# Channel-major tiles for the convolved columns, and the convolution beside the tile that follows each

## The reference, cut to what matters

```python
(m_qk, m_v, m_o, m_gate, m_if, a_q, a_k, a_v, a_gate,
 i_q, i_w, i_k, c_q, c_gate) = split_in(rms_norm(x, g_pre) @ w_in)     # m_qk: 2048 columns
qk, conv_state = causal_conv(m_qk, zeros, conv_w, conv_b)   # 4 taps per channel along the tokens, then SiLU
m_out, (C, n, m) = mlstm_mixer(qk, m_v, m_o, m_if, b_if, head_norm, carry0, MLSTM_CHUNK)  # 4 heads x 256
# beside it: sparse attention over selected keys, and attention over 256 memory tokens
y = x + rms_norm(concat(m_out * silu(m_gate), a_out * ..., c_out * ...) @ w_out, g_post)
```

## Time and profile before

| what | value |
|---|---|
| median of 3 runs | 1882.44 us (1881.62 to 1884.41) |
| the profiled execution | 1877.01 us, its span 1875.3 us |
| granted TensorE clock over the span | 0.937 of full speed |
| second group, last tile read at | 1256.8 us |
| numerators of heads 0 to 3 begin | 1391.1, 1461.0, 1529.6, 1580.3 us |
| tiles of the output projection begin | 1647 us |

### The profile page before, as it was taken

The page is one execution under the profiler, slowest core; times in us unless marked ns, Lnnn a source line. Parts: engine busy times, 40 slices in busy tenths (PEclk is TensorE's granted clock), DMA queues, the critical chain, the costliest instruction groups (busy, mean ns, idle before and its releaser), DMA issues.

```text
span 1875.3 us, 20980 instructions
## 1 busy us (share of the span) xinstructions
PE 1679.8 (90%) x7801; PEld 1272.0 (68%) x7801; DVE 814.8 (43%) x1319; ACT 569.1 (30%) x876; POOL 673.4 (36%) x448
## 2 busy tenths in 40 slices
PE   6899999999999499998899999987658789799995
PEld 5677775677897376776688778865334455477774
DVE  6400010599929856755632161112465454501113
ACT  5522233222221233233222422224244443312221
POOL 3655531333333166766444444421110111033331
PEclk9999999999999699999999999998667788789997
DMA  6544431233344267766455544437404323542222
GB/s 214 160 134 130 142 101 56 71 105 108 92 120 144 77 196 231 221 197 211 122 154 165 149 134 117 147 125 230 93 29 152 107 68 107 192 160 85 83 78 106
DMA packets 139674, 249.01 MB, mean 133 GB/s; under 512 B 26504, under 2 KB 63308, under 8 KB 136296
## 3 DMA queue, kind: packets, MB, share of 16 engines
q10 hardware_dynamic: 66928, 122.86, 21.0%
q1 hardware_dynamic: 55920, 72.76, 12.2%
q0 software_dynamic: 16736, 52.18, 9.6%
HBM read 204.11 MB, written 43.66 MB: 132 GB/s over the span
## 4 chain that ended last, share of the span: by engine, by line
PE 73%; DVE 13%; DMA 5%; ACT 4%; issue 2%; POOL 1%; ACTq 1%; SPq 0%; DVEq 0%; POOLq 0%
PE acc L431 16%; PE acc L433 16%; PE acc L432 16%; PE acc L426 4%; PE acc L427 4%; PE ps_c L991 3%; PE acc L1722 2%; DVE arena L1669 1%; PE ps_c L2116 1%; PE acc L2111 1%; DMA arena<-z_prompt 1%; PE ps_a L1155 1%; POOL w_lo L389 1%; ACT z_tile L471 1%; PE ps_a L1224 1%
## 5 line engine op out<-in xcount | busy, mean ns | idle before, releaser
L389 POOL TENSOR_TENSOR w_lo<-w_raw,w_hi 128x1024 fp32r<-128x1024 f32 (+1 forms) x200 | 466.7, 2334 | 814.8 <-ACT w_hi L385 814.5
L431 PE MATMUL acc<-w_hi,x_hi 128*128 128x512 f32 (+1 forms) x1472 | 580.4, 394 | 8.8 <-DVE keep L925 5.3
L433 PE MATMUL acc<-w_hi,x_lo 128*128 128x512 f32 (+1 forms) x1472 | 565.9, 384 | 0.0
L432 PE MATMUL acc<-w_lo,x_hi 128*128 128x512 f32 (+1 forms) x1472 | 565.3, 384 | 0.0
L385 ACT CAST w_hi<-w_raw 128x1024 fp32r<-128x1024 f32 (+1 forms) x200 | 204.2, 1021 | 758.3 <-PE acc L427 716.6
L431 PEld LDWEIGHTS acc<-w_hi,x_hi 128*128 128x128 f32 x1472 | 278.8, 189 | 93.9 <-issue 28.0
L433 PEld LDWEIGHTS acc<-w_hi,x_lo 128*128 128x128 f32 x1472 | 278.1, 189 | 55.8
L432 PEld LDWEIGHTS acc<-w_lo,x_hi 128*128 128x128 f32 x1472 | 278.8, 189 | 51.4 <-issue 0.7
L426 PE MATMUL acc<-w_hi,x_hi 128*64 128x512 f32 (+1 forms) x368 | 141.4, 385 | 0.0
L427 PE MATMUL acc<-w_lo,x_hi 128*64 128x512 f32 (+1 forms) x368 | 140.9, 384 | 0.0
L2231 DVE TENSOR_TENSOR arena<-arena (+1 forms) x16 | 14.0, 887 | 176.8 <-ACT arena L464 176.8
(11 more groups left out here) (439 smaller groups left out, 1903.0 us busy)
## 6 DMA issues: line engine op xcount, KB each, us to landing
w_raw<-in_w_in ACTq DMA_DIRECT2D x136, 512.0 KB, 3.7
z_prompt<-z_tile ACTq DMA_DIRECT2D x68, 256.0 KB, 2.5
w_raw<-in_w_out ACTq DMA_DIRECT2D x32, 512.0 KB, 3.6
arena<-z_prompt SPq DMA_DIRECT2D x4, 2088.0 KB, 10.2
w_raw<-in_w_mem_kv ACTq DMA_DIRECT2D x16, 512.0 KB, 4.1
arena<-q_sample POOLq DMA_DIRECT2D x32, 256.0 KB, 4.0
arena<-z_prompt SPq DMA_DIRECT2D x10, 512.0 KB, 7.3
between<-z_prompt SPq DMA_DIRECT2D x10, 512.0 KB, 10.1
```

The source lines that it names most:

```text
L389: nc.gpsimd.tensor_tensor(out=w_lo[:, c % 2, :, 0:w], in0=w_raw[:, c % RAWS, :, 0:w], in1=w_hi[:, c % 2, :, 0:w].bitcast(F32), op=ALU.subt ...
L431: nc.tensor.matmul(acc[m][:, 0:w], xh, wh, start=first, stop=False)
L432: nc.tensor.matmul(acc[m][:, 0:w], xh, wl, start=False, stop=False)
L433: last = nc.tensor.matmul(acc[m][:, 0:w], xl, wh, start=False, stop=end)
```

## The change

The ten tiles of the second group are taken in another order, with the four convolved ones as the fifth to eighth. In these four, PE takes the weights as the stationary operand and the tokens as the moving one, so that a PSUM bank holds 128 channels by 512 tokens. ACT copies the bank to `z_tile` without scaling. Beside the tile that follows, DVE multiplies by the tokens' RMS factors (spread over all partitions at the start), keeps the last three tokens, and applies the taps; ACT takes SiLU after that tile's sixth chunk and stores 128 channels by 512 tokens to a new scratch `qk_prompt`. The heads load q and k from there, already turned and convolved. The tap weights are loaded with the first tables and turned between two tiles of the first group. `p_conv` is written from the kept tokens, in six DMAs of 4-byte elements.

```diff
+    B_ORDER = (4, 5, 6, 7, 0, 1, 2, 3, 8, 9)
 def tensor_tile
+                            if kind == "t":
+                                xh, xl = hi_t[:, k, 0:S], lo_t[:, k, :]
+                                wh, wl = (v[:, c % 2, i, m * P:(m + 1) * P] for v in (w_hi, w_lo))
+                                nc.tensor.matmul(acc[m][:, :], wh, xh, start=first, stop=False)
+                                nc.tensor.matmul(acc[m][:, :], wl, xh, start=False, stop=False)
+                                last = nc.tensor.matmul(acc[m][:, :], wh, xl, start=False, stop=end)
+                                continue
 def scalar_evacuate
+                if kind == "t" and m < MT:
+                    nc.scalar.copy(z_tile[:, m, :], acc[m][:, :]).then_inc(acc_read, 1)
+                    continue
 def scalar_tile
+                if c == CH - 2 and late is not None:
+                    late()
+        def tensor_late_consts(pe):
+            pe.wait_ge(*at("rstd_spread"))
+            pe.wait_ge(tables_in, 16 * N_TABLES)
+            for m in range(MT):
+                nc.tensor.matmul(ps_c[:, m * P:(m + 1) * P], conv_a[:, m * P:(m + 1) * P], ident[:, :], start=True, stop=True)
+            for k in range(KT):
+                last = nc.tensor.transpose(ps_b[:, k * (CK + 1):(k + 1) * (CK + 1)], conv_nat[:, k * P:(k + 1) * P],
+                                           ident[0:CK + 1, 0:CK + 1])
+        def vector_conv(dve, i, m):
+            k = 4 * i + m
+            dve.wait_ge(acc_read, acc_base(N_B0 + CT0 + i) + m + 1)
+            dlink(nc.vector.tensor_tensor(out=conv_a, in0=z_tile[:, m, :], in1=rstd_bc, op=ALU.mult))
+            nc.vector.tensor_copy(last_rows(k // 8)[:, k % 8, :], conv_a[:, S - CK + 1:S])
+            out = z_tile[:, m, :]
+            dlink(nc.vector.tensor_scalar(out, conv_a, conv_c[:, k, CK - 1:CK], None, ALU.mult))
+            for j in range(1, CK):
+                ins = nc.vector.scalar_tensor_tensor(out=out[:, j:S], in0=conv_a[:, 0:S - j],
+                                                     scalar=conv_c[:, k, CK - 1 - j:CK - j], in1=out[:, j:S],
+                                                     op0=ALU.mult, op1=ALU.add)
...
+        def scalar_conv(act, i):
+            for m in range(MT):
+                act.wait_ge(cv_tapped, k + 1)
+                nc.scalar.activation(z_tile[:, m, :], z_tile[:, m, :], ACT.Silu, bias=conv_c[:, k, CK:CK + 1]).then_inc(cv_silu, 1)
+            for m in range(MT):
+                act.wait_ge(cv_silu, k + 1)
+                act.dma_start(qk_p[k * P:(k + 1) * P, :], z_tile[:, m, :]).then_inc(z_stored[m], 16)
+        def sync_conv_state(sp):
+            sp.wait_ge(cv_tapped, 4 * NCT)
+            for half in range(2):
+                for j in range(CK - 1):
+                    sp.dma_start(O["p_conv"][0, 0, j, half * MW:(half + 1) * MW].rearrange("(k p) -> p k", p=P),
+                                 last_rows(half)[:, :, j], allow_slow_non_contiguous=True).then_inc(conv_out, 16)
 def sync_mlstm_head
-            for i, c in enumerate((C_QK, C_QK + MW, C_O, C_G, C_V)):
+            for i in range(2):
+                src = qk_p[i * MW + h * MD:i * MW + (h + 1) * MD, :].rearrange("(d p) t -> p d t", p=P)
+                sp.dma_start(qk_t[h % 2][:, i, :, :], src).then_inc(zh_in[h % 2], 16)
+            for i, c in enumerate((C_V, C_O, C_G)):
 def tensor_mlstm_head
-            pe.wait_ge(conv_silu, 4 * (h + 1))
+            pe.wait_ge(zh_in[h % 2], zh_count(h))
...
-                if h + 1 < H:
-                    tensor_conv_turn(pe, h + 1, i)
 block.vector, the loop over the second group's chunks
-            for _ in range(CH * NBT):
+            for i in range(CH * NBT):
                 next(prompt, None)
                 next(rows, None)
                 next(prompt, None)
+                t = i // CH - CT0 - 1
+                if 0 <= t < NCT and i % CH < MT:
+                    vector_conv(dve, t, i % CH)
```

More of the change, by code:

```diff
@@ L58, in hybrid_decoder_step @@
     NBT = C_IF // TN
+    NCT = 2 * MW // TN
+    B_ORDER = (4, 5, 6, 7, 0, 1, 2, 3, 8, 9)
+    CT0 = B_ORDER.index(0)
+    assert len(B_ORDER) == NBT and B_ORDER[CT0:CT0 + NCT] == tuple(range(NCT))
     N_Y0 = N_B0 + NBT
@@ L491, in tile_loop, with scalar_tile @@
                 body(n0 + 1)
-        def scalar_tile(act, n, kind, steps=NO_STEPS, often=False):
+        def scalar_tile(act, n, kind, steps=NO_STEPS, often=False, late=None):
             for c in range(1, CH + 1):
@@ L566, in hybrid_decoder_step @@
         gate_s = keep[:, 912:1040]
+        CK = 4
+        conv_nat = place(X_OFF, [2 * MW], CK + 1)
+        conv_a = place(X_OFF + 3112, [S])
+        conv_c = conv_cols[:, :].rearrange("p (k j) -> p k j", j=CK + 1)
+        last_rows = lambda half: small[:, 32 * half:32 * half + 24].rearrange("p (k j) -> p k j", j=CK - 1)
         POOL_PAGES = 2 * CH * IXT
@@ new lines, in vector_late_consts @@
+        def vector_late_consts(dve):
+            dve.wait_ge(rstd_ready, 2)
+            for m in range(MT):
+                last = nc.vector.tensor_copy(conv_a[:, m * P:(m + 1) * P], rstd(NU_MEM + m, P).broadcast_to([P, P]))
+            last.then_inc(reached("rstd_spread"), 1)
+            dve.wait_ge(*at("late_turned"))
+            nc.vector.tensor_copy(rstd_bc, ps_c[:, :])
+            nc.vector.tensor_copy(conv_c, ps_b[:, 0:KT * (CK + 1)].rearrange("p (k j) -> p k j", j=CK + 1)
+                                  ).then_inc(reached("late_copied"), 1)
+            dve.wait_ge(*at("late_copied"))
@@ L1462, in hybrid_decoder_step @@
         c_e = keep_m[:, 40:60].rearrange("p (m h) -> p m h", h=H)
[L1463 to L1475, removed]
+        mx_T = keep_m[0:H, 60:70]
+        bias_g = keep_m[0:H, 70:72]
+        m0_s = keep_m[0:H, 72:80]
+        a_T = keep_m[0:H, 80:88]
+        bn_o = keep_m[:, 88:96]
+        st_m = keep_m[:, 96:104]
+        aT8 = keep_m[0:NB, 104:108]
+        w_b = keep_m[0:R, 108:140].rearrange("p (h b) -> p h b", h=H)
+        batch_of = keep_m[0:R, 140:148]
+        head_rows = sb("head_rows", [P, H * P])
+        hr = head_rows[0:H, :]
+        rstd_bc = head_rows[:, :]
+        z_h = [place(M0, [2, MT, MD]), part(xl_free, 0, [2, MT, MD])]
         va = [place(M0 + 5120, [MT, MD + 2]), part(xl_free, 4096, [MT, MD + 2])]
         qk_t = [place(M0 + 7180, [2, 2, S]), part(xl_free, 5128, [2, 2, S])]
-        cv = [place(M0 + 6152, [S]), place(M0 + 6668, [S])]
         k_n = place(M0 + 9228, [MT, MD])
@@ L2429, in _ @@
             for n in range(N_B0, N_Y0):
-                scalar_tile(act, n, "b", steps)
+                i = n - N_B0
+                scalar_tile(act, n, tile_kind(n), steps,
+                            late=(lambda i=i: scalar_conv(act, i - CT0 - 1)) if CT0 < i <= CT0 + NCT else None)
             run(steps[0])
@@ L2469, in _ @@
             run(mem_s)
-            for u in range(4):
-                vector_conv(dve, 0, u)
             prep, pairs = vector_mlstm_s_prep(dve), vector_mlstm_s(dve)
@@ L2498, in _ @@
             for n in range(N_B0, N_Y0):
-                tensor_tile(pe, n, "b", steps)
+                tensor_tile(pe, n, tile_kind(n), steps)
             run(steps[0])
```

115 lines of the change are left out of this document (37 added, 78 removed).

## The result

The changed kernel takes 1860.14 us (median of 4 runs, 1854.18 to 1865.89), the kernel before 1883.43 beside it (4 runs); ratio 0.9875, 95% interval 0.9841 to 0.9909. It is faster by 23 us where 42 were forecast. The time lies inside the range that I gave, 2 us from its upper end, and outside the forecast's own 1828 to 1853. So places are compared inside the executions, and totals by the medians.

The account below looks back on a forecast made before the run. PE was taken to bound the second group, a chain of single waits the heads. Heads gain 55 us, the second group costs 13: 42 off the 1882.4 median gives 1840; own ends 1828 to 1853, range 1822 to 1862.

Parts of the forecast that it names:

- slower than before: Rival: p_conv's 4-byte stores, priced 25 us on SP's queue, delay the heads' constants and loads; 1885 or more, chance 0.04.
- The heads: Convolution units leave the heads: 18 us to head 0's numerator, 36 in heads 1 and 2, 1 in the memory stage; 55.
- 18 + 1: Head 0's numerator 18 us earlier (2.5 at the start, then 16.0), plus 1 from weights and constants turned before the memory stage.
- the 16.0: Inside head 0: four gains summed as head 1's units no longer alternate with the sample rows' preparation.
- the 36: Heads 1 and 2: both numerator spacings fall to head 3's 50.7, 37.1 us, taken as 36; bounds nothing and 37.1.
- The heads refill: Rival: DVE's normalisation, states' loads or table loads keep heads 1 and 2 near 60 us; 1858, chance 0.12.
- spacings over 58: Sign against the forecast: numerators of the heads over 58 us apart, where near 51 was expected.
- The second group: Added cost of 13 us: turned constants 2, sixth tile 8, seventh tile 2, ninth tile 1.
- 4 to 13: Sixth tile: bounds of an 8 us cost, as two convolutions are queued on DVE ahead of the sample rows' softmax.
- The turned constants: Before the index stage: four 128-wide products and 16 small ones cost PE 2 us; DVE's copies lie in a wait.
- the exchange of operands: Second group: matmuls and weight loads keep number and shape, only which operand stands still changes; priced 0.
- PE waits in the second group that sum to over 30: Sign against the forecast: PE's waits there total over 30 us; a 10 to 15 us softmax wait was expected.

Follow-up runs that it names:

- the store mended: Against the changed kernel, kept tokens are turned on PE, copied by ACT and stored as 48 rows of 512 bytes; 1838.05 us, 0.9774 of the kernel before.
- e_spread: Changed kernel with the six stores' 4-byte elements written 512 bytes apart in a scratch, p_conv itself not written; 1837.70 us, 0.9765 of the kernel before.

## Why the prediction was right and where it was wrong

**`p_conv`: the step that failed.** Under "slower than before" I gave the stores 25 us on the DMA engines, looked for who is queued behind them on SP's queue, found the heads' constants, and put the price at nothing: "over long before the constants are asked for near 1266". The length was near (some 31 to 35 us). What failed is that I asked only who stands behind them on SP's queue: a gather on GpSimd's queue lands after 34.9 us and weights on ACT's after 34.2, and PE wants the gather 15.8 us after its issue, so it stands for 19.1. It cost 22 us (1860.1 to 1838.1 with the store mended; 19 by the ratios). The mean of 65 ns a packet was no measure of it either: spread, the same elements cost PE no wait.

**The heads: the mechanism right, 9 us too large.** The first sample add waits for its load, 9.9 us (worked out: 10.2), and hides head 0's own units. From the tenth tile's read to head 0's numerator it is 124.9 us, before 139.5: 14.6 gained, forecast 18 + 1. Of the 4.4 that are missing 3.0 lie before the first sample add, which comes 0.5 us sooner after that read (89.5 for 90.0) and not 2.5 + 1: its loads are issued 1.9 us later (79.2 for 77.3), which no run explains. Inside head 0 14.2 of the 16.0 came. The spacings of heads 1 and 2 went from 69.9 and 68.6 to 51.6 and 55.8: 31.1 of the 36. What is missing here is one stretch at the lower clock. After, in head 2:

```profile
1482.00:1492.00 10.00, 10.00 (x21) 4.21 (x20) 2.23 (x5) 1.90 (x6) 0.00 (x0) 0.50 1.02 338
```

In `e_spread` it lies in head 1, and the spacings there are 55.6 and 50.8:

```profile
1408.00:1418.00 10.00, 10.00 (x24) 4.64 (x22) 2.20 (x5) 1.36 (x4) 0.00 (x0) 0.50 1.02 333
```

Ten us at 0.50 with PE full are 5 us of work. Wherever heads 1 and 2 await no load, one of the two takes 55.6 to 55.8 us and the other 50.8 to 51.6. Why it falls for so long in the one head or the other no run here shows. "The heads refill" at 60 us was wrong; spacings over 58, the sign against me, did not come up.

**The second group without the stores: right, 6 us too dear.** With them left out the tenth tile is read 7.1 us later than before (1258.7 for 1251.6), forecast 13. The sixth tile pays 4.2 us (70.3 for 66.1), at the lower end of 4 to 13: PE's wait is 10.7, in the 10 to 15 that I said would show it, and the edit that moves the convolutions behind the softmax takes it away again. The seventh and eighth tile pay nothing (76.5 and 76.5; 77.4 and 77.4), forecast 2 and 0; the ninth 1.5 (82.7 for 81.1), forecast 1. By the rule of the Trainium skill on the shared port (SBUF — State Buffer), and if each convolution met a subtraction of GpSimd, this tile would have lost some 12. The groups of after by shape (busy us, mean ns) show less:

```profile
L709 DVE SCALAR_TENSOR_TENSOR z_tile<-arena,conv_cols,z_tile 128x510 f32<-128x510 f32 x16 | 14.0, 876 | 0.6
L704 DVE TENSOR_TENSOR arena<-z_tile,head_rows 128x512 f32<-128x512 f32 x16 | 12.2, 763 | 2.7 <-ACT z_tile L482 2.4
...
L705 DVE COPY small<-arena 128x3 f32<-128x3 f32 x16 | 4.7, 296 | 0.5
```

Against the medians of the lines (750, 692 and 169 ns) that is 16 x (126 + 71 + 127) ns = 5.2 us for all sixteen. That is three instructions, in the rows from 923.1, 941.8 and 1015.9, each beside a subtraction of GpSimd (start, us):

```profile
922.60 2.66 POOL L394 TENSOR_TENSOR w_lo<-w_raw,w_hi 128x1024 fp32r<-128x1024 f32 x1 [2.92 <-ACT w_hi L390]
...
923.10 2.19 DVE L705 COPY small<-arena 128x3 f32<-128x3 f32 x1
```

The other thirteen convolutions lie between two subtractions or touch one by under 0.2 us. So the two do exclude each other where they meet, two of the three with both inputs in SBUF as the rule has it, the third a copy with one; wrong was that each meets one.

**The turned constants: right.** They stand between the third and the fourth tile's read of the first group: 87.8 us, 85.6 before, the 2 that I priced, and without the stores the group ends 2.2 later (556.4). After ends it 5.5 later: 1.4 come from the start, and some 2 from a stretch in which the clock falls. It falls so in one other execution, the one with a single store, whose group ends at 559.4; the rest end it at 556.1 to 557.6:

```profile
330.00:340.00 10.00, 8.20 (x24) 4.01 (x23) 0.68 (x1) 3.97 (x7) 2.35 (x1) 0.83 0.37 112
```

**Nothing for the exchange of operands: right.** From read to read the fifth, seventh and eighth tile, whose operands are exchanged, take 68.3, 76.5 and 77.4 us, and the tiles at these places took 68.7, 76.5 and 77.4.

**The sum: near by luck in part.** The heads gained 45.7 of the 55, and the second group cost 7.1 of the 13: 9 us too much and 6 too much take each other back, and inside the executions 38 of the 42 are left without the stores (1875.3 to 1837.0). The medians give 43, because the profiled run of before (1877.0) lies below the medians of before (1881 to 1883). And the forecast's own ends don't come out of its terms: with the heads at 55 the bounds of the second group (6 to 26) give 1833 to 1853, not 1828, and the heads' bound of no gain in heads 1 and 2 is left out.

**A sign set badly.** "PE waits in the second group that sum to over 30" was to show me wrong. From 640 us to the group's end they sum to 53.6 after; but before they sum to 29.2, so the 10 to 15 that I expected in place of 5.3 would have passed the mark by themselves.

## What to carry to other kernels

A store of single elements that lie side by side in DRAM and come from many partitions can hold the loads of other queues too, here a gather by 30 us, and half as many hold it nearly as long; turn such data on chip first and store rows. When a transfer is called hidden, list every wait for any DMA in that stretch with the time from its issue to its use: the smallest of them (15.8 us here) is the cover, not that of the store's own queue. Work put in an engine's idle time goes behind, not ahead of, the one step that another engine awaits in that tile.

## What the runs showed of the hardware that was not expected

- 3072 writes of 4 bytes side by side in DRAM leave the core 34 GB/s for 24 us (128 without them; 17 packets in one stretch of 3 us); 6144 of them 512 bytes apart go out in 12 us beside other traffic, and 16 bytes apart they hold the gather by 6.7 us.
- The stall isn't proportional: 8.5, 27.6 and 30.2 us on a gather for one, three and six rows of 4 KB. With one it goes on for some 9 us after the last element has gone out.
- SP's issue is held too: 40.2 us for the six, against 8.4 to 10.0 us when the elements lie apart (issued in head 0 it is 11.7, and the loads behind them are held instead); its line shows a single one of 28.1 us (ns min/median/max):

```profile
L1601 SPq DMA_DIRECT2D out_p_conv<-small x6: 433/651/28134, 1212.4 to 1243.1; - x6
```
